# Six gather slots per expert table in place of eight, and the space used for weight chunks of the expert queries loaded during the mixer

## The reference

```python
def one_block(xblk):
    q = (xblk @ w_query).reshape(B, TOKEN_BLOCK, N_PEER_HEADS, 2, SUBKEY_DIM)
    s = jnp.einsum('bthpd,hpnd->bthpn', q, sub_keys).astype(jnp.float32)
    vals, idx = lax.top_k(s, PEER_TOPK)
    cand = (vals[..., 0, :, None] + vals[..., 1, None, :]).reshape(...)
    cand_idx = (idx[..., 0, :, None] * N_KEYS + idx[..., 1, None, :]).reshape(...)
    top_s, pos = lax.top_k(cand, PEER_TOPK)
    eidx = jnp.take_along_axis(cand_idx, pos, axis=-1)
    g = jax.nn.softmax(top_s, axis=-1).astype(xblk.dtype)
    u = expert_u[eidx]
    h = jnp.einsum('btd,bthkd->bthk', xblk, u)
    act = jax.nn.gelu(h, approximate=False) * g
    return jnp.einsum('bthk,bthkd->btd', act, expert_v[eidx])
```

## Time and profile before

| | |
|---|---|
| median of 3 runs | 3475.18 us (3475.16 to 3476.74) |
| the profiled execution | 3474.13 us, its span 3472.3 us |
| mean granted TensorE clock | 0.982 |
| busy: PE, PEld, DVE, ACT, POOL | 92%, 70%, 71%, 48%, 33% of the span |
| moved by DMA | 936.98 MB, mean 270 GB/s |

### The profile page before, as it was taken

How to read it: one execution, slowest core, us unless ns; L and a number is a source line. 1 busy time by engine, 2 the same in 40 slices (tenths; PEclk the granted TensorE clock), 3 DMA queues, 4 the chain that set the end, 5 groups by cost and what they waited for, 6 DMA issues and landing times. The chain is left out here.

```text
span 3472.3 us, 48317 instructions
## 1 busy us (share of the span) xinstructions
PE 3179.6 (92%) x16922; PEld 2415.9 (70%) x16922; DVE 2466.0 (71%) x4772; ACT 1667.5 (48%) x3730; POOL 1139.9 (33%) x1243
## 2 busy tenths in 40 slices
PE   6998989988789798898977999999999999999999
PEld 5995444443279754444423888999988888999988
DVE  7876666766677566667675777867687877867686
ACT  3743333333366433333333555756554655756553
POOL 1306667777613176677774000002000000002000
PEclk8999999999999999999999999999999999999999
DMA  8789999999976699999998554444466554444565
GB/s 312 235 288 366 409 409 409 409 409 409 396 250 207 231 409 409 409 409 409 409 409 321 164 183 145 140 140 135 158 188 188 178 186 140 140 140 138 157 187 163
DMA packets 258286, 936.98 MB, mean 270 GB/s; under 512 B 29312, under 2 KB 30720, under 8 KB 257792
## 3 DMA queue, kind: packets, MB, share of 16 engines
q0 software_dynamic: 161280, 587.27, 43.0%
q1 hardware_dynamic: 96768, 346.62, 31.1%
HBM read 932.73 MB, written 1.05 MB: 269 GB/s over the span
## 5 line engine op out<-in xcount | busy, mean ns | idle before, releaser
L824 PE MATMUL M<-rows,diag 128*128 128x512 f32 x2048 | 969.9, 609 | 192.8 <-DMA rows<-in_expert_v_dram,expert 163.2
L1346 DVE CUSTOM_DVE_ANT_0 rows<-rows,G 128x1024 f32<-128x1024 f32 x512 | 616.7, 1219 | 425.5 <-DMA rows<-in_expert_u_dram,expert 342.4
L824 PEld LDWEIGHTS M<-rows,diag 128*128 128x128 f32 x2048 | 366.1, 191 | 744.9 <-DMA rows<-in_expert_v_dram,expert 411.1
L334 DVE TENSOR_TENSOR w_low<-ring,w_high 128x1024 fp32r<-128x1024 f32 x560 | 689.9, 1235 | 245.9 <-ACT w_high L326 227.0
L326 ACT ACTIVATE w_high<-ring 128x1024 fp32r<-128x1024 f32 x560 | 590.8, 1057 | 251.9 <-PE G L417 133.5
L544 POOL DMA_INDIRECT rows<-in_expert_u_dram,expert x512 | 482.2, 942 | 340.7 <-DVE expert L1329 140.7
L544 POOL DMA_INDIRECT rows<-in_expert_v_dram,expert x512 | 481.9, 941 | 187.3 <-issue 122.2
L353 PE MATMUL G<-x_halves,w_high 128*128 128x256 f32 x1360 | 400.5, 294 | 4.1 <-DVE w_low L334 3.9
L356 PE MATMUL G<-x_halves,w_low 128*128 128x256 f32 x1360 | 385.8, 284 | 0.0
L1054 ACT ACTIVATE diag<-const,weight 128x128 f32<-128x128 f32 x512 | 198.3, 394 | 271.3 <-PE M L824 270.3
L355 PE MATMUL G<-x_halves,w_high 128*128 128x256 f32 x1104 | 314.4, 285 | 0.0
(11 more groups left out here) (408 smaller groups left out, 6123.2 us busy)
## 6 DMA issues: line engine op xcount, KB each, us to landing
ring<-in_stream_dram SPq DMA_DIRECT2D x632, 512.0 KB, 3.5
ada_ring<-in_ada_stream_dram POOLq DMA_DIRECT2D x80, 512.0 KB, 4.8
rows<-in_ada_stream_dram POOLq DMA_DIRECT2D x16, 512.0 KB, 16.4
rows<-in_expert_u_dram,expert POOLq DMA_INDIRECT x512, 16.0
rows<-in_expert_v_dram,expert POOLq DMA_INDIRECT x512, 16.0
ada_ring<-in_stream_dram SPq DMA_DIRECT2D x8, 512.0 KB, 5.3
spare<-in_stream_dram SPq DMA_DIRECT2D x6, 512.0 KB, 6.9
sq<-in_stream_dram SPq DMA_DIRECT2D x4, 512.0 KB, 9.3
```

Source lines behind the costliest of these rows:

```text
L334: dve.tensor_tensor(T["w_low"][:, part, :], T["ring"][:, place.slot(chunk, slots), :], T["w_high"][:, part, :].bitcast(F32), ALU.subtract) ...
L824: mm = pe.matmul(M[:, 2 * t + half, :], T["diag"][:, n % 4, :], T["v_rows"][:, n % SLOTS, half * 512:(half + 1) * 512], start=(h == 0 and ...
L1346: dve.tensor_tensor_reduce(row, row, TOKENS, 1.0, 0.0, ALU.mult, ALU.add, T["hid"][:, r, k:k + 1]).then_inc(sem["u_used"], 1)
```

## The change

`SLOTS` becomes 6. The slots of both tables are now the first 12 x 1024 floats of `rows`. The upper quarter of `rows` (`va[4D:8D]`) is free in the expert stage, and `va[0:4D]`, which are now slots 2 to 5 of table v, is free until the first gathers. The 16 tiles of modulation weights that open layer 0 keep 16 slots (`FIRST_SLOTS` = 8 a table). `key_score` keeps the scores of 4 heads in place of 8 (slot h % 4), so the upper half of `gates` is free too.

`SPARE` becomes 17: 4 in `va[4D:8D]`, 2 in `attn`, 2 in the upper half of `gates`, 4 in `ada_ring`, 2 in `sq`, 3 in tiles of their own. Four more chunks, 53 to 56 (`EARLY`), go to `va[0:4D]`. TensorE takes them for the first queries, after one wait for all four (`x_loaded`). The ring's numbering skips them: ring load 53 is chunk 57, and the last, 67, is chunk 71. So 21 of the queries' 36 chunks pass the ring by.

SyncE's program in the mixer is now: ring loads up to 46, then 4 spares (after `pooled`), 47 and 48, 2 spares (after the attention's low halves), 49, 2 spares (after the last pool projection is read), 50 to 55, in layer 1 the 4 of `ada_ring`, then the 4 early chunks (after all attention projections), 56 to 58, in layer 0 the 4 of `ada_ring`, then after the mean square the last 5 spares. GpSimd waits for the end of the first queries (`G_FIRST_END`) before the gather of row 2 of table v.

```diff
@@ -46,7 +46,9 @@
 PEER_HEADS, N_KEYS, TOPK = 8, 128, 16
 N_EXPERTS = N_KEYS * N_KEYS
 ROUNDS = PEER_HEADS * TT
-SLOTS = 8
+SLOTS = 6
+FIRST_SLOTS = 8
+KEY_HEADS = 4
 SUB = 4
 PAIR = 2
 N_ADA = 6
...
@@ -70,9 +72,11 @@
 TILES_1 = (T_IN * KD + 4 + 4 * KD + 2 * KD * KD
            + PEER_HEADS * (4 * KD + 4))
 CHUNKS_1 = -(-TILES_1 // TILES)
-SPARE = 11
+SPARE = 17
 RING_CHUNKS = CHUNKS_1 - SPARE
 MIX_CHUNKS = -(-(T_IN * KD + 4 + 4 * KD + 2 * KD * KD) // TILES)
+
+EARLY = range(MIX_CHUNKS, MIX_CHUNKS + 4)
 
 
 PAR_1 = {}
...
@@ -232,7 +238,17 @@
         tiles = []
         for _ in range(n):
             chunk, r = divmod(self.at, TILES)
-            slot = self.place.slot(chunk, self.slots)
+            if self.early and chunk in EARLY:
+                if chunk == EARLY[0] and r == 0:
+                    self.pe.wait_ge(self.early_loaded, 16 * (1 + len(EARLY) * self.spare_turn))
+                tiles.append(self.early[chunk - EARLY[0]][:, r * P:(r + 1) * P])
+                self.at += 1
+                continue
+            if self.early and chunk >= EARLY[0]:
+                chunk_in_ring = chunk - len(EARLY)
+            else:
+                chunk_in_ring = chunk
+            slot = self.place.slot(chunk_in_ring, self.slots)
             if self.spare and chunk >= RING_CHUNKS:
                 n = chunk - RING_CHUNKS
                 if r == 0:
...
@@ -242,7 +258,7 @@
                 continue
             if r == 0:
 
-                self.pe.wait_ge(self.loaded[slot], 16 * (chunk // self.slots + 1))
+                self.pe.wait_ge(self.loaded[slot], 16 * (chunk_in_ring // self.slots + 1))
             tiles.append(self.ring[:, slot, r * P:(r + 1) * P])
             self.at += 1
         return tiles
...
@@ -474,7 +490,8 @@
 
     def row_turn(n):
 
-        return 16 * (1 + (layer * ROUNDS * TOPK + n) // SLOTS + 1)
+        before = -(-(ROUNDS * TOPK - n % SLOTS) // SLOTS)
+        return 16 * (1 + layer * before + n // SLOTS + 1)
 
     def ada_turn(n):
...
@@ -509,17 +526,49 @@
                 sp.wait_ge(sem["ada_step"], KD)
                 for chunk in range(RING):
                     load_chunk(sp, T["stream1"], layer, CHUNKS_1, ring, sem["w_loaded"], chunk, order=ORDER_1)
-            in_mixer = MIX_CHUNKS + RING - 1
             load_weights(sp, T["stream1"], layer, CHUNKS_1, ring, sem["w_loaded"], sem["w_used"], order=ORDER_1,
-                         last=in_mixer)
-            sp.wait_ge(sem["ada_step"], len(parts) * KD)
-            for n in range(SPARE):
-                if n == ADA_RING:
-                    sp.wait_ge(sem["norm_full"], F_NORM + 1)
-                sp.dma_start(T["spare"][n], T["stream1"][layer * CHUNKS_1 + RING_CHUNKS + n]
-                             ).then_inc(run["c_then_spare_loaded"], 16)
-            load_weights(sp, T["stream1"], layer, CHUNKS_1, ring, sem["w_loaded"], sem["w_used"], order=ORDER_1,
-                         first=in_mixer, last=RING_CHUNKS)
+                         last=EARLY[0] - RING)
+
+            def load_spare(first, last):
+                for n in range(first, last):
+                    sp.dma_start(T["spare"][n], T["stream1"][layer * CHUNKS_1 + RING_CHUNKS + n]
+                                 ).then_inc(run["c_then_spare_loaded"], 16)
+
+            def behind_early(ring_chunks):
+
+                for at in ring_chunks:
+                    before = at - RING
+                    sp.wait_ge(sem["w_used"], before + 1 + (len(EARLY) if before >= EARLY[0] else 0))
+                    sp.dma_start(ring[:, at % RING, :], T["stream1"][layer * CHUNKS_1 + at + len(EARLY)]
+                                 ).then_inc(sem["w_loaded"][at % RING], 16)
+
+            for at in range(EARLY[0] - RING, EARLY[0]):
+                sp.wait_ge(sem["w_used"], at - RING + 1)
+                load_chunk(sp, T["stream1"], layer, CHUNKS_1, ring, sem["w_loaded"], at)
+                if at == EARLY[0] - RING:
+                    sp.wait_ge(sem["pooled"], 4)
+                    load_spare(0, 4)
+                if at == EARLY[0] - RING + 2:
+                    sp.wait_ge(sem["x_low_ready"], 2 * KD)
+                    load_spare(4, 6)
+                if at == EARLY[0] - RING + 3:
+                    evacuated_1(sp, g_free, G_POOLO + KD - 1)
+                    load_spare(6, 8)
+            behind_early(range(EARLY[0], EARLY[0] + 3))
+            if not opening:
+                sp.wait_ge(sem["ada_step"], len(parts) * KD)
+                load_spare(8, 12)
+            sp.wait_ge(g_full, G_ATTO + KD)
+            for n, chunk in enumerate(EARLY):
+                sp.dma_start(T["early"][n], T["stream1"][layer * CHUNKS_1 + chunk]
+                             ).then_inc(run["x_loaded"], 16)
+            behind_early(range(EARLY[0] + 3, EARLY[0] + RING - 1))
+            if opening:
+                sp.wait_ge(sem["ada_step"], len(parts) * KD)
+                load_spare(8, 12)
+            sp.wait_ge(sem["norm_full"], F_NORM + 1)
+            load_spare(12, SPARE)
+            behind_early(range(EARLY[0] + RING - 1, RING_CHUNKS - len(EARLY)))
 
             if not opening:
                 sp.wait_ge(run["cleared"], 1)
...
@@ -541,6 +590,8 @@
                 n = r * TOPK + k
                 if n >= SLOTS:
                     pool.wait_ge(used, n - SLOTS + 1)
+                elif buf is T["v_rows"] and n == 2:
+                    pool.wait_ge(g_full, G_FIRST_END)
                 pool.indirect_dma_start(
                     buf[:, n % SLOTS, :], None, table,
                     bass.IndirectOffsetOnAxis(ap=T["expert"][:, r, k:k + 1], axis=0)
...
@@ -602,15 +653,16 @@
                 if n >= behind:
                     r, k = divmod(n - behind, TOPK)
                     gather(T["expert_v"], T["v_rows"], rows["v_landed"], sem["v_used"], r, k)
-            for n in range(SLOTS):
-
-                pool.wait_ge(rows["u_landed"][n], row_turn(ROUNDS * TOPK - SLOTS))
-                pool.wait_ge(rows["v_landed"][n], row_turn(ROUNDS * TOPK - SLOTS))
+            for n in range(ROUNDS * TOPK - SLOTS, ROUNDS * TOPK):
+
+                pool.wait_ge(rows["u_landed"][n % SLOTS], row_turn(n))
+                pool.wait_ge(rows["v_landed"][n % SLOTS], row_turn(n))
 
         @block.tensor
         def _(pe):
             w = WeightStream(pe, ring, sem["w_loaded"], sem["w_used"], spare=T["spare"],
-                             spare_loaded=run["c_then_spare_loaded"], spare_turn=layer + 1)
+                             spare_loaded=run["c_then_spare_loaded"], spare_turn=layer + 1, early=T["early"],
+                             early_loaded=run["x_loaded"])
 
             heads, parts_read = [0], [0]
...
@@ -1291,7 +1343,7 @@
                 if part < 2:
                     p = part
                     evacuated_1(dve, g_free, g_scores(h, t))
-                    s = T["key_score"][:, h, (2 * t + p) * P:(2 * t + p + 1) * P]
+                    s = T["key_score"][:, h % KEY_HEADS, (2 * t + p) * P:(2 * t + p + 1) * P]
                     link(dve.max(out=val[:, p, 0:8], in_=s))
                     dve.max_index(out=idx[:, p, 0:8], in_max=val[:, p, 0:8], in_values=s)
                     link(dve.match_replace(out=rest[:, 0:N_KEYS], in_to_replace=val[:, p, 0:8],
...
@@ -2686,10 +2738,11 @@
             with ExitStack() as scope_rows:
                 first = scope_rows
 
-                both = sb1("rows", 2 * SLOTS * D)
-                ua, va = both[:, 0:SLOTS * D], both[:, SLOTS * D:]
-                T1["ada_first"] = part(both, 0, 2 * SLOTS, D)
-                T1["u_rows"], T1["v_rows"] = part(ua, 0, SLOTS, D), part(va, 0, SLOTS, D)
+                both = sb1("rows", 2 * FIRST_SLOTS * D)
+                ua, va = both[:, 0:FIRST_SLOTS * D], both[:, FIRST_SLOTS * D:]
+                T1["ada_first"] = part(both, 0, 2 * FIRST_SLOTS, D)
+                T1["u_rows"], T1["v_rows"] = part(both, 0, SLOTS, D), part(both, SLOTS * D, SLOTS, D)
+                T1["early"] = [va[:, n * D:(n + 1) * D] for n in range(len(EARLY))]
                 T1["qk"] = part(ua, 0, UNITS, S)
                 T1["probs"] = part(ua, 2560, 2, TT, S)
                 T1["probsT"] = part(ua, 3584, 2, TT, S)
...
@@ -2710,11 +2763,13 @@
                 T1["expert"] = sb1("expert", ROUNDS, TOPK, dt=U32)
                 for name in ("neg_top", "gate_sum", "gate_inv"):
                     T1[name] = sb1(name, ROUNDS)
-                T1["spare"] = [T1["ada_ring"][:, n, :] for n in range(ADA_RING)]
-                T1["spare"] += [sb1(f"spare{n}", TILES * P)[:, :] for n in range(SPARE - ADA_RING - 4)]
                 squares = T1["sq"][:, :, :].rearrange("p k t -> p (k t)")
-                T1["spare"] += [squares[:, n * TILES * P:(n + 1) * TILES * P] for n in range(2)]
-                T1["spare"] += [att[:, n * TILES * P:(n + 1) * TILES * P] for n in range(2)]
+                T1["spare"] = [va[:, n * D:(n + 1) * D] for n in range(4, 8)]
```

(21 more changed lines are left out.)

## The result

| | before | changed |
|---|---|---|
| median of the runs | 3475.19 us (3475.16 to 3476.74, 4 runs) | **3457.01 us** (3455.86 to 3457.75, 4 runs) |
| ratio, 95% interval | | 0.9947 (0.9935 to 0.9959) |
| the profiled execution, its span | 3474.13 us, 3472.3 us | 3455.86 us, 3454.1 us |
| mean granted TensorE clock | 0.982 | 0.982 |
| stage of layer 0, layer 1 | 689.06, 688.58 us | 679.37, 679.72 us |

18.2 us less; 3457.3 was predicted. "Stage" is from the issue of a layer's first gather to the landing of its last, read from the trace. The stages are 9.69 and 8.86 us shorter, 18.5 us together: all of the gain.

What follows compares the result with a forecast made beforehand. DMA transfers at 409 GB/s bound the expert stages; 14 fewer chunks save 17.9 us, six slots and mixer loads cost 0, so 3475.2 - 17.9 = 3457.3 us, range 3452 to 3467.

Steps and rivals of the forecast that it cites:

- What bounds the kernel: Expert stages of both layers: DMA transfers at 409 GB/s are the bound; one chunk or gather costs 1.28 us.
- Part 1: Expert stages: 7 fewer ring chunks among the gathers, 8.97 us a layer, 17.9 us in both.
- The inner bound: Round 0 of the expert stages: the seventh chunk (63) gains nothing, a loss of 2.6 us for both layers.
- Part 2: Gathers with six slots a table: least lead falls from 13.8 to 8.7 us, 6.6 needed; cost 0.
- Part 3: Last third of the mixer: 12 more chunks loaded in idle DMA time; cost 0, at worst 5.1 us a layer.
- A: Expert stages: seventh chunk and some cover lost, gain 15.4 us, 3459.8 us; chance 0.84 together with the forecast.
- B: Expert stages: six slots starve the DMA, each tight round loses 5.1 us, 82 in all, 3539 us; chance 0.06.
- C: Mixers give the gain back: exposed bursts and late early chunks, 22.6 us back, 3480 us; chance 0.03.
- D: Expert stage: PE is the true bound, only 0 to 5 us won, 3472 us; chance 0.06.
- E: Expert stages: each removed DMA is worth more than its bytes, 4.5 us, 63 us in all, 3412 us; chance 0.01.
- the forecast's second rival: Expert stages, the same as B: six slots starve the DMA, 3539 us; chance 0.06.
- outer bound of 13.8 us of lead: Gathers, within B: full rate needs the 13.8 us least issue-to-landing time, so each tight round loses 5.1 us.

Runs made afterwards that it cites:

- the angles spread: Changed kernel, six slots, with the rope angles' operations handed out in pairs behind rows 9 to 14 of rounds 2 and 3: 3457.91 us.
- the burst of eight: Changed kernel with the first eight spare chunks loaded in one burst behind ring load 49, not as 4, 2 and 2: 3456.50 us.

## Why the prediction was right

The total came within 0.3 us of the forecast. That close is luck: the four runs span 1.9 us, and the size of one chunk was off by 0.04 us as below. The mechanism is another matter.

**What bounds the kernel.** Right. Seven chunks a layer are gone and the stage is shorter by their bytes at an unchanged 409 GB/s. By the Trainium skill (DMA: Bandwidth & Descriptors, Specifications), whose limit is about 358 GB/s a core, the estimate was 20.5 us; the traces show 409 GB/s in both kernels and 18.2 us. That row is a stack's rate divided by two cores; here one core ran.

**Part 1.** Right in size and in place: 18.4 / 14 = 1.32 us a chunk from the two kernels (1.18 if the 1.9 us of six slots alone are real and theirs), 1.26 from three chunks put back, 1.5 from the seventh alone, where 1.28 was counted. The inner bound, that the seventh chunk might be worth nothing in round 0, is contradicted by the kernel without early chunks.

**Part 2.** Cost 0 was right: six slots alone change nothing. The arithmetic of the lead was right as well (8.7 and 10.9 forecast, 8.7 and 11.0 measured there). Two details failed. First, the tightest place: I looked at the token turns and in round 0, and took the minimum of before as the place that would stay tightest. In the changed kernel the least lead from 320 us on is 7.6 us, behind `rope_angles`, which I had not looked for; with the angles spread it is 8.7 again. Second, the view of the earlier trace rows began at 320 us. In the view of 300 to 320 us the least time to landing was 11.6 us before, not 13.8, and less 5.1 that is 6.5, below the 6.6 that I took as needed. In the changed kernel it is 7.8 there in the first profile and 7.2 in the second. "The cover is thinnest in round 0" pointed near this place without a number. None of it cost anything, but the margin of 2.1 us over 6.6 was in truth 0.6 to 1.0. The place matters once slots are scarcer: five slots lose 1.9 us at 300 to 330 us. The needed lead of 6.6 us was on the safe side: with five slots the leads of 437 to 930 us have a median of 7.9 and a least value of 6.1 us, at 408 GB/s, and layer 1's stage, with the same least lead, is as short as with six. With a median of 6.6 us the rate is 367 to 392 GB/s.

**Part 3.** Cost 0 was right, and PE was busy throughout. The ring load behind the burst of four landed after 8.4 us where 9.1 was worked out; the longest behind a spare burst took 9.1. That the limit lies at 11.6 us was too strict a reading: a load of 12.5 us made ScalarE wait and still cost PE nothing. The early chunks of layer 1 were to have landed at 1178.1, that is 1168.5 with the 9.6 us by which the program had moved, and 2.2 us ahead of the first queries; they landed at 1169.8, 0.9 us ahead. The closest place was named rightly, and its cover was thinner than worked out. The first gather was issued at 270.56 us, 1.1 us earlier than before where 1 us was allowed; over the profiles of the other kernels it lies between 269.9 and 272.2, so this says little.

**The rivals.** A (the seventh chunk lost) fell with the kernel without early chunks. B needed four slots, not six. C was tried with the burst of eight and gave nothing back. D is out, as the DMA stays at 409 GB/s and PE's busy share rises. E is out: 1.2 to 1.5 us a chunk is its bytes and little more, not 4.5 or 3.2. The 3.2 was in any case worked out for the wrong issuer: the Trainium skill (DMA: Bandwidth & Descriptors, Anatomy of one DMA) gives its 2.0 us plus bytes for a DMA issued by GpSimd, and the removed chunks were SyncE's.

## What to carry to other kernels

When a stage is bound by the rate of transfers, count its bytes and move those that are known early to a stretch in which the DMA has room; what it saves is bytes over the measured rate, here 17.9 us worked out and 18.2 measured. Slots for data in flight are worth only the lead that they give: compare the lead of the trace with the one at which the rate was last full, and sell the rest. Look for the tightest place at the longest stretch in which nothing is released, an odd piece of other work between two rounds included, and not at the regular waits alone.

## What the runs showed of the hardware

The fall was softer than the forecast's second rival had it, with its outer bound of 13.8 us of lead. With 6 and 6 slots the gathers' lead is 7.6 us at least and 10.5 at the median, and the rate is 409 GB/s; with 5 and 5, at a median of 8.0 and a least value of 6.1 from 437 us on, it is 408 except at two places, and layer 1's stage is no longer than with 6 and 6; with 4 and 4, at 6.6, it is 367 to 392 GB/s, and the two stages are 38 and 30 us longer. Each slot less in both tables took about 2.5 us of the median (11.0 with six alone, from 16.0 with eight; 10.5 to 8.0 with five), until at four the gathers simply came late. And a wait for a DMA in the records need not cost anything: 2.4 us of it at ScalarE took the place of 2.5 us of waiting for PE.
